# Two transformer blocks on one core: most of the 128x128 transposes taken off TensorE and done by VectorE in 32x32 blocks with a trip through DRAM

## What is computed

```
h   = rmsnorm(x);  proj = h @ w_in                      # 2048 -> 9216
u, v_sgu, q, k, v, g_a, g_b = split(proj)
y_a = gelu(u) * spatial_gating(rmsnorm(gelu(v_sgu)))    # 8 groups of 128
y_b = stick_breaking_attention(rmsnorm(q), rmsnorm(k), v)   # 8 heads
x  += (sigmoid(g_a)*(y_a @ w_up_a) + sigmoid(g_b)*(y_b @ w_up_b)) @ w_o
x  += (silu(gate)*up) @ w_ffn_out,   [gate, up] = rmsnorm(x) @ w_ffn_in   # 5632 wide
x  += sigmoid(rmsnorm(x) @ w_ple_gate) * (p @ w_ple)
# second block
z   = rmsnorm(x) @ w_in2                                # 3584 columns: conv, pool, q
kv  = rmsnorm(mem) @ w_kv
x  += concat(conv(z), pool(z), attention(q, kv)) @ w_out
u   = causal_dwconv(rmsnorm(x) @ w_up2, 3 taps) + bias  # 2 x 5632 columns
x  += (silu(gate)*val) @ w_down
out = rmsnorm(x)
```

## Time and profile before

| what | value |
|---|---|
| time, median of 3 runs (lowest to highest) | 2510.04 us (2508.74 to 2510.11) |
| time of the profiled execution itself | 2509.36 us |
| its span, first to last instruction | 2507.2 us |
| TensorE busy | 2486.9 us, 99% |
| VectorE busy | 1403.4 us, 56% |
| ScalarE busy | 1244.4 us, 50% |
| DMA, mean of 16 engines | 62.2% on the queue of the weights, 189 GB/s |
| granted TensorE clock | 0.999 of full |

### The profile page before, as it was taken

One profiled execution on the slowest core, in us unless ns is written; L12 is line 12 of the kernel. 1 busy time (PEld: TensorE's weight loads), 2 busy tenths in 40 slices (PEclk: granted clock), 3 DMA queues, 4 the chain that ended last, 5 costly groups with the idle time before them and its releaser, 6 DMA issues.

```text
span 2507.2 us, 27926 instructions
## 1 busy us (share of the span) xinstructions
PE 2486.9 (99%) x11322; PEld 2065.1 (82%) x11322; DVE 1403.4 (56%) x1668; ACT 1244.4 (50%) x1531; POOL 0.2 (0%) x4
## 2 busy tenths in 40 slices
PE   9999999999999999999999999999999999999998
PEld 7888888888888888888888788888888888888886
DVE  7564555655555455544445654765566665665544
ACT  7554666445444444444445654444555555554443
POOL 0000000000000000000000000000000000000000
PEclk9999999999999999999999999999999999999999
DMA  8656666666666666666666565566666666666663
GB/s 287 185 180 188 193 187 178 192 185 185 187 191 189 189 190 188 192 186 192 192 189 225 171 186 178 168 190 186 180 191 185 184 184 191 185 184 209 194 193 128
DMA packets 131105, 473.55 MB, mean 189 GB/s; under 512 B 14624, under 2 KB 15008, under 8 KB 130720
## 3 DMA queue, kind: packets, MB, share of 16 engines
q1 hardware_dynamic: 130976, 471.77, 62.2%
HBM read 469.61 MB, written 2.10 MB: 188 GB/s over the span
## 4 chain that ended last, share of the span: by engine, by line
PE 98%; ACT 1%; DVE 1%; DMA 0%; issue 0%; SPq 0%; DVEq 0%; ACTq 0%
PE ps L1291 86%; PE ps L1297 8%; PE ps L374 2%; ACT wh L1327 0%; DMA raw<-in_w_in 0%; DVE wl L1328 0%; PE ps L732 0%; PE ps L703 0%; PE ps L748 0%; PE ps L580 0%; PE ps L958 0%; PE ps L994 0%; DVE X L881 0%; DVE tmp L876 0%; PE ps L705 0%
## 5 line engine op out<-in xcount | busy, mean ns | idle before, releaser
L1328 DVE TENSOR_TENSOR wl<-raw,wh 128x1024 fp32r<-128x1024 f32 x877 | 1074.0, 1225 | 1076.9 <-ACT wh L1327 1076.6
L1327 ACT CAST wh<-raw 128x1024 fp32r<-128x1024 f32 x877 | 922.6, 1052 | 1171.4 <-PE ps L1297 1168.1
L1291 PE MATMUL ps<-wh,x1g_hi 128*128 128x512 f32 x704 | 276.1, 392 | 0.0
L1291 PE MATMUL ps<-wh,x4g_hi 128*128 128x512 f32 x704 | 276.0, 392 | 0.0
L1291 PE MATMUL ps<-wh,act_hi 128*128 128x512 f32 x704 | 274.3, 390 | 0.0
L1291 PE MATMUL ps<-wl,x1g_hi 128*128 128x512 f32 x704 | 274.0, 389 | 0.0
L1291 PE MATMUL ps<-wl,x4g_hi 128*128 128x512 f32 x704 | 273.9, 389 | 0.0
L1291 PE MATMUL ps<-wl,act_hi 128*128 128x512 f32 x704 | 273.9, 389 | 0.0
L1291 PE MATMUL ps<-wh,h_hi 128*128 128x512 f32 x576 | 227.0, 394 | 2.3 <-DVE wl L1322 1.3
L1291 PE MATMUL ps<-wl,h_hi 128*128 128x512 f32 x576 | 224.1, 389 | 0.0
L1291 PE MATMUL ps<-wh,x1g_lo 128*128 128x512 f32 x528 | 205.7, 390 | 0.0
(11 more groups left out here) (271 smaller groups left out, 3147.4 us busy)
## 6 DMA issues: line engine op xcount, KB each, us to landing
raw<-in_w_in SPq DMA_DIRECT2D x200, 512.0 KB, 3.6
raw<-in_w_ffn_in SPq DMA_DIRECT2D x176, 512.0 KB, 3.6
raw<-in_w_up SPq DMA_DIRECT2D x176, 512.0 KB, 4.2
raw<-in_w_ffn_out SPq DMA_DIRECT2D x88, 512.0 KB, 3.6
raw<-in_w_down SPq DMA_DIRECT2D x88, 512.0 KB, 3.6
raw<-in_w_o SPq DMA_DIRECT2D x32, 512.0 KB, 3.6
raw<-in_w_ple_gate SPq DMA_DIRECT2D x32, 512.0 KB, 3.6
raw<-in_w_out SPq DMA_DIRECT2D x32, 512.0 KB, 3.6
```

Of the source, the lines that this page charges most:

```text
L1291: return e.matmul(*a, start=s, stop=p, skip_group_check=True)
L1327: hi = act.do(lambda e, r=r, slot=slot: e.copy(wh[:, r, :], raw[:, slot, :]), in_tok[s], free)
L1328: lo_tok[s] = dve.do(lambda e, r=r, slot=slot: e.tensor_tensor(wl[:, r, :], raw[:, slot, :], wh[:, r, :].bitcast(F32), ALU.subtract), hi)
```

## The change

- `turn` no longer uses TensorE. Two VectorE instructions transpose the 32x32 blocks of the chunk's rows into a new buffer `Y` [128 x 1024]; one DMA on GpSimd's queue writes `Y` to a DRAM scratch tensor `rows` (two of them in turn, 512 KB each); GpSimd's queue waits for that, and four more DMAs (one for each group of 32 partitions, 128 KB each in pieces of 1 KB) read it back into a new buffer `Z` so that every feature lies on its partition. The VectorE instructions wait until the previous turn's write has left `Y`, the four reads until the previous turn's readers are done with `Z`.
- The readers take their tiles from `Z` in SBUF, through strided views with pieces of 32 elements, in two halves of 128 tokens each. They stand later: step +6 in `unfold` (turn at +1), +7 in `after_u` and `after_z` (turn at +1), +10 in `after_qk` (turn at +4), +8 in `after_ub` and `after_ffn1` (turn at +1), +7 in `after_ffn2` (turn at +1).
- `turn_now` is the old way, kept for 5 turns of 67: the last chunk of `unfold` of three of the four norms, the last of `after_ub`, and chunk 6 of `after_z`.
- `after_ffn1` turns two chunks together (11 turns of 8 tiles in place of 22 of 4). `after_ffn2` first copies `Z` into `Y` on ScalarE (two instructions of 128x512), the taps then read `Y`.
- The two new buffers take 8 KB per partition, so RAW goes from 6 to 4. Some functions move by 2 to 5 steps (`sgu_pair`, `xhead`, `pool_tile`, `conv_taps`, `conv_split`), the order of `w_out`'s granules changes, and the first chunk of `after_ffn1`, `after_pgate` and `after_ffn2` is no longer 2 or 3 steps late.

```diff
-RAW = 6
+RAW = 4
...
-MIX_ORDER = (12, 14, 0, 6, 2, 8, 10, 4)
+MIX_ORDER = (12, 14, 0, 6, 8, 10, 2, 4)
...
+        Y = view("Y", [P, 1024], o_y)
+        Z = view("Z", [P, 1024], o_z)
+        YF = Y.rearrange("p (c t) -> p c t", c=4)
+        YQ = Y.rearrange("p (q g c j) -> p q g c j", q=4, g=2, c=4)
+        ZT = Z.rearrange("p (a g c j) -> p c g a j", a=4, g=2, c=4)
+        ZA = Z.rearrange("p (a e) -> p a e", a=4)
...
-        def turn(src, tok, bk, n):
-
-            done = None
-            for c in range(n):
+        turned = {"n": 0, "y": [], "z": []}
+        def turn(src, *tokens):
+            n = turned["n"]
+            turned["n"] += 1
+            for b in range(2):
+                done = dve.do(lambda e, b=b: e.transpose(YQ[:, :, b].rearrange("p q c j -> p c q j"),
+                                                         src[:, b, :].rearrange("p (c q j) -> p c q j", c=4, q=4)),
+                              *tokens, turned["y"])
+            there = moves.load(s_rows[n % 2], rows_out[n % 2], Y[:], done)
+            for q in range(4):
+                back = moves.load(s_turn[n % 4], ZA[32 * q:32 * q + 32],
+                                  rows_out[n % 2, :, 256 * q:256 * q + 256].rearrange("(a i) e -> i a e", a=4),
+                                  there, turned["z"])
+            turned["y"] = there
+            turned["rows"] = done
+            return back
+        def split_turned(dest, c, tok):
+            for h in range(2):
+                hi_, lo_ = (tiles(x[:, c:c + 4, :])[:, :, h] for x in (dest.hi, dest.lo))
+                hi = act.do(lambda e, o=hi_, h=h: e.copy(o, ZT[:, :, h]), tok)
+                lo = dve.do(lambda e, o=lo_, i=hi_, h=h: e.tensor_tensor(o, ZT[:, :, h], i.bitcast(F32), ALU.subtract), hi)
+            turned["z"] = lo
+            for k in range(c, c + 4):
+                dest.ready[k] = lo
+        def turn_now(src, tok, bk):
+            for c in range(4):
                 for b in range(2):
                     at_ = (c % 2) * T + b * P
                     done = pe.do(lambda e, c=c, b=b, at_=at_: e.transpose(
                         ps[:, bk + c // 2, at_:at_ + P], src[:, b, c * P:(c + 1) * P], ident[:]),
-                        tok, bank_free[bk], bank_free[bk + 1] if n > 2 else None, got_mats["ident"])
+                        tok, bank_free[bk], bank_free[bk + 1], got_mats["ident"])
             return done
-        def turned(bk, c):
+        def turned_tile(bk, c):
             return ps[:, bk + c // 2, (c % 2) * T:(c % 2 + 1) * T]
+        def tiles(x):
+            return x.rearrange("p c (g a j) -> p c g a j", g=2, a=4)
...
-            bk = 6 if norm is norm4 else 4 + 2 * (n % 2)
             g = {}
+            xs = X[:, :, 512 * n:512 * n + 512]
+            soon = n == 3 and norm is not norm4
 
             def a():
                 squares(n, tok, norm)
+                if not soon:
+                    g["t"] = turn(xs, tok)
 
             def b():
-                g["t"] = turn(X[:, :, 512 * n:512 * n + 512], tok, bk, 4)
+                if soon:
+                    g["t"] = turn_now(xs, tok, 6)
                 for i in range(4):
                     c = 4 * n + i
-                    hi = act.do(lambda e, c=c, i=i: e.activation(dest.hi[:, c, :], turned(bk, i), ACT.Copy,
-                                                                 scale=gain(gname, c)), g["t"], free())
-                    if i % 2 == 0:
+                    src = turned_tile(6, i) if soon else ZT[:, i:i + 1]
...
-            at(s + 2, b)
+            at(s + (2 if soon else 6), b)
...
-                    g["t"] = st_tok["free"] = turn(ST, g["st"], bk, 4)
+                    g["t"] = turn(ST, g["st"])
+                    st_tok["free"] = turned["rows"]
                 hi = act2.hi[:, 2 * n:2 * n + 2, :].rearrange("p k t -> p (k t)")
                 lo = act2.lo[:, 2 * n:2 * n + 2, :].rearrange("p k t -> p (k t)")
 
                 def a():
-                    g["c"] = [act.do(lambda e, c=c: e.activation(C[:, c, :], F[:, c, :], ACT.Identity,
+                    for h in range(2):
+                        g["f"] = act.do(lambda e, h=h: e.copy(tiles(YF)[:, :, h], ZT[:, :, h]), g["t"])
+                    g["c"] = [act.do(lambda e, c=c: e.activation(C[:, c, :], YF[:, c, :], ACT.Identity,
                                                                  scale=gain("fconv", 176 + 4 * n + c),
-                                                                 bias=gain("fbias", 4 * n + c)), g["t"], part_tok["tb"])
+                                                                 bias=gain("fbias", 4 * n + c)), g["f"], part_tok["tb"])
                               for c in range(4)]
+                    turned["z"] = g["f"]
 
                 def b():
                     g["o"] = []
                     for c in range(4):
                         o = dve.do(lambda e, c=c: e.scalar_tensor_tensor(
-                            C[:, c, 1:], F[:, c, 0:T - 1], gain("fconv", 88 + 4 * n + c), C[:, c, 1:],
+                            C[:, c, 1:], YF[:, c, 0:T - 1], gain("fconv", 88 + 4 * n + c), C[:, c, 1:],
                             ALU.mult, ALU.add), g["c"][c])
                         g["o"].append(o)
                     for c in range(4):
                         g["o"][c] = dve.do(lambda e, c=c: e.scalar_tensor_tensor(
-                            C[:, c, 2:], F[:, c, 0:T - 2], gain("fconv", 4 * n + c), C[:, c, 2:],
+                            C[:, c, 2:], YF[:, c, 0:T - 2], gain("fconv", 4 * n + c), C[:, c, 2:],
                             ALU.mult, ALU.add), g["o"][c])
-                    bank_free[bk] = bank_free[bk + 1] = [g["c"], g["o"]]
+                    turned["y"] = [g["c"], g["o"]]
...
-                w = 3 if n == 0 else 0
-                at(s + w, z)
-                at(s + w + 2, y)
+                z()
+                at(s + 1, y)
                 for i, fn in enumerate((a, b, c_, d, f, h)):
-                    at(s + w + 2 + i, fn)
+                    at(s + 7 + i, fn)
```

More of the change, by code:

```diff
@@ L230, in two_block_kernel @@
             "s_attn", "s_cst", "s_mats", "s_misc", "s_late", "s_mem", "s_out", "s_ident", "s_x", "s_gf"))
+        s_turn = [sem(f"s_turn{i}") for i in range(4)]
+        s_rows = [sem(f"s_rows{i}") for i in range(2)]
+        rows_out = nc.dram_tensor("rows", (2, P, 1024), F32, kind="Internal").ap()
         sp = Queue(sem("s_sp"))
@@ L402, in b @@
-                bank_free[bk] = bank_free[bk + 1] = [hi, dest.ready[c]]
+                    src = turned_tile(6, i) if soon else ZT[:, i:i + 1]
+                    as_src = (lambda v, c=c: v[:, c, :]) if soon else (lambda v, c=c: tiles(v[:, c:c + 1, :]))
+                    hi = act.do(lambda e, c=c, s=src, f=as_src: e.activation(f(dest.hi), s, ACT.Copy, scale=gain(gname, c)),
+                                g["t"], free())
+                    if soon and i % 2 == 0:
+                        first = (c, src, as_src)
+                        continue
@@ new lines, in b @@
+                    for c, src, as_src in ((first, (c, src, as_src)) if soon else ((c, src, as_src),)):
+                        for h in range(1 if soon else 2):
+                            half = (lambda v: v) if soon else (lambda v, h=h: v[:, 0, h])
+                            dest.ready[c] = dve.do(lambda e, c=c, s=src, f=as_src, h=half: e.scalar_tensor_tensor(
+                                h(f(dest.lo)), h(s), gain(gname, c), h(f(dest.hi).bitcast(F32)), ALU.mult, ALU.subtract),
+                                hi)
@@ L547, in b, with c @@
                 def b():
[L548 to L552, removed]
[L553 to L554 removed]
+                    g["t"] = turn(rows, g["u"])
+                    rows_tok[n] = turned["rows"]
+                def c():
+                    u_tok[n] = turned["z"] = [act.do(lambda e, h=h: e.copy(tiles(U[:, 4 * n:4 * n + 4, :])[:, :, h],
+                                                                           ZT[:, :, h]), g["t"]) for h in range(2)]
+                a()
+                at(s + 1, b)
+                at(s + 7, c)
             return after
@@ L638, in f, with h @@
                 def f():
[L639 to L644, removed]
+                    g["t"] = turn(rows, g["r"])
+                    rows_tok[n] = turned["rows"]
+                def h():
+                    turned["z"] = [act.do(lambda e, h=h: e.activation(tiles(dst[:, 4 * n:4 * n + 4, :])[:, :, h],
+                                                                      ZT[:, :, h], ACT.Copy, scale=g_ap),
+                                          g["t"], got_mats["gq"]) for h in range(2)]
+                    qk_tok.append(turned["z"])
                 a()
@@ L782, in after, with now @@
                 m = dve.do(lambda e: e.tensor_tensor(ST, ST, SG[:, n, :, :], ALU.add), tok, ua_tok[n])
+                g = {}
                 def a():
-                    done = st_tok["free"] = turn(ST, m, bk, 4)
```

(13 more changed lines are left out.)

108 lines of the change are left out of this document (59 added, 49 removed).

## The result

| | before | changed |
|---|---|---|
| median of 4 runs | 2509.46 us | 2567.64 us (2564.22 to 2573.86) |
| ratio | | 1.0235, 95% interval 1.0214 to 1.0255 |
| the profiled execution, and its span | 2509.36, 2507.2 us | 2573.86, 2572.0 us |

The change makes the kernel 2.3% slower, where 2460 us were forecast. It is the rival on the other side: the round trip became the bound of `w_up2`. The profiled execution of the changed kernel is the slowest of its four, 6.2 us above their median; the kernel before repeats within 1.4 us, the changed one within 10 us.

The account below looks back on a forecast made before the run. It took TensorE's instruction stream as the bound: 2509.4 - 56.9 (transposes) - 3.4 (a wait in the ple stage) + 7 (loop) + 3 (`w_out`'s start) = 2459.1, forecast as 2460 us; range 2449 to 2500 us.

Parts of the forecast that it names:

- the rival on the other side: In `after_ffn2`, the DMA trip becomes the bound and the change loses, for example 2528 us at 14.5 us; chance 12%.
- The loop: In `after_ffn2`, turn, trip, copies, taps, next turn once a chunk: 10.9 us plus R against 21.77; about 7 us lost.
- R: The DMA round trip, from the end of the transposes to the landing of the fourth read.
- I take R = 11.2 us: Trip estimate: 5.5 us for the write, as loads of `X`, and 5.7 for the reads, as `BS`.
- The bounds of 7.2 and 19.8: Trip limits: two legs of 3.6 us below; two of 9.9 us, as the 2 MB load, above.
- the 2452 without a loop: Whole kernel's time in us if the trip is hidden, R up to 10.9; that rival's chance 30%.
- hidden altogether: Rival: R up to 10.9, no loop in `after_ffn2`; 2452 us, or 2449 if `w_out`'s start is free; 30%.
- the other stages cost nothing: Trips in `unfold`, `after_z`, `after_u` and `after_qk` costed at nothing; `unfold` allowed about 16 us before TensorE stands.
- the cushion of 5 us: In `unfold`, ring slack of some 5 us beyond the 11.0 us of trip allowed for nothing.
- The weights rival: With four raw buffers, loads beside trips come late, 1 to 2 us in each of 62 turns; about 2490 us; 7%.
- The point of no gain: In `after_ffn2`, the loop takes back the 57.3 us won, 2.7 us in each of 21 periods, from R = 13.6.
- The 3 us for the start of `w_out`: Around `w_out`'s start, conv products, taps and pool splits come closer together on VectorE: 3 us (0 to 6).

Follow-up runs that it names:

- experiment 5: The changed kernel, with each weight load of `w_up2` fetching 64 of 1024 columns (wrong weights, same instructions and waits): 2472.20 us, ratio 0.9855.
- experiment 6: The changed kernel with taps reading a separate copy, placed behind the next chunk's turn in `w_up2`, plus 64-column weight loads there: 2473.03 us, ratio 0.9853.
- experiment 2: The kernel before, with RAW = 4 in place of 6 and nothing else: 2508.97 us, ratio 0.9999.
- experiment 3: The changed kernel, with the two VectorE transposes of each turn in `w_up2` made twice: 2548.11 us, ratio 1.0160.
- experiment 9: The changed kernel, with the weight load issued ahead of each `w_up2` trip's write held until that write has landed: 2542.84 us, ratio 1.0135.
- experiment 8: The changed kernel with `w_up2` turned on TensorE, and the readers of `unfold` at step +8 in place of +6: 2468.40 us, ratio 0.9838.
- experiment 1: The changed kernel, with the 22 turns of `w_up2` made on TensorE as before and taps reading PSUM: 2481.07 us, ratio 0.9887.
- experiment 4: The changed kernel, with the taps' copy in its own memory and the VectorE taps behind the next chunk's turn in `w_up2`: 2493.95 us, ratio 0.9933.

## Why the prediction was wrong, point by point

**Right.** TensorE was the bound, and its transposes cost what was read: without them a chunk of `w_up2` takes 21.77 us where nothing else interferes (experiments 5 and 6). A transpose pair on VectorE takes 1.30 us (1.3 taken). RAW = 4 costs the kernel before nothing (experiment 2). The loop is there, its fixed part is 10.94 us (10.9 taken), and it binds when R exceeds 10.9: periods of 21.76 us at R = 8.4, 26.48 at 15.5.

**Wrong: the size of R.** The step that failed is "I take R = 11.2 us". It was 15.6 in the loop shown, 15.5 in the median. Both legs were too small: 6.2 us for the write in place of 5.5, and 9.2 for the reads in place of 5.7; 0.3 us lie between the transposes and the write. The bounds of 7.2 and 19.8 held, and so did the arithmetic of the loop: 21 x (26.5 - 21.77) = 99 us on top of the 2452 without a loop gives 2551.

Beside small loads the legs are 3.25 and 5.1 us, R is 8.6 us (experiment 5); so 7.0 of the 15.6 us are the weights beside it. The reads were the larger miss, 3.5 of 4.4 us. I had taken four DMAs in a row from `BS`, which stood in the weights' own queue with small ones ahead of it. Here the four issues alone take 2.2 us, and the last landed 7.5 us after its issue. What was beside them is seen in the loads: seven were issued from 1956.0 to 1967.6, one in 1.9 us in place of 2.72, because ScalarE and VectorE catch up after each wait, just where the trip runs. I took this bunching at first for the whole cause, a late trip bunching the loads that make the next one late. That it is not: with the loop open the write leg was as long. Nor can it make most of R: beside `w_ffn_in`, where TensorE's pace is steady, R is 12.9 us, which is already 2.0 over the 10.9. By that R the loop would cost 21 x 2.0 = 42 us, an estimate; what is between 12.9 and 15.5 may be bunching or where the trip falls between two loads; no run parts these. Experiments 3 and 9 show what the write leg is worth: 3.2 to 3.5 us with the load ahead landed or about to, about 6 with it just begun. Experiment 9 also shows that this can't simply be had, since reads and weights then take part of it back.

The Trainium skill's figure for a DMA from GpSimd ("DMA: Bandwidth & Descriptors", Anatomy of one DMA: about 2.0 us and bytes/436e3, so an estimate of 3.2 us for 512 KB) agrees with the trace where only loads of 32 KB run beside it, 3.25 us. It does not hold beside the stream, 6.2 us. The R near 7 that I worked out from it would have put the change into the case "hidden altogether", and was not used in the sum.

**Wrong: the other stages cost nothing.** I let R be up to 16 us in `unfold` for nothing. Experiment 8 against 1 says 12.7 us between the medians; in the profiled execution of the changed kernel `w_up2` starts 20.2 us later than in that of experiment 8. The stage rows show where: between the first matmul of x2g and of x3g the kernel before took 153.2 us (1341.6 to 1494.8), the changed one 158.2, that of experiment 8 143.5. ScalarE waited up to 7.7 us for a trip, with its casts queued behind, and the cushion of 5 us that I had worked out for one wait did not hold in the ple stage. `w_ffn_in`, too, took 483.6 us in place of 489.1, while experiment 8 has 479.0, which is 22 x 21.77. TensorE has no gap in it from 620 us on, so the trips inside it cost nothing, as forecast, and the loss stands at its start, behind `unfold`. That the steps of the ple stage are fuller, with the split of `mem` put down in the same ones, is my reading; no run takes it apart.

**The weights rival** was in part right, and hidden by the loop. In the changed kernel ScalarE waited 49.6 us for the raw weights of `w_up2`, in gaps that the loop left anyway. With the loop opened it is what is left: 2494 us against 2473 with small loads, 21 us (experiments 4 and 6).

**The point of no gain was misplaced with it.** The prediction put it at R = 13.6, from 57.3 us won. Without the loop's loss the changed kernel takes 2472 us (experiment 5), so only 37 us were won, and the change loses from R = 10.9 + 37 / 21 = 12.7 us on. Experiment 9 fits that: R = 14.3 gives 2472 + 21 x 3.4 = 2543 us, and 2542.8 was measured.

**The sum by what the runs showed**, by place, against the profiled execution of 2573.9: 2449 without loop and extras, 20.2 ahead of `w_up2` (1738.1 against 1717.9 in experiment 8), 94.9 inside it (573.8 against 478.9), 8.5 behind it, makes 2573. The loop as a whole is 21 x (26.5 - 21.77) = 99 us from the first to the last turn; its last period ends behind the stage's last matmul, so a part of the 8.5 us is the same loss. The 3 us for the start of `w_out` were too much: from first to last start its matmuls take 91.0 us, 92.5 before with three groups of transposes among them, so about 1 us was lost.

## What to carry to other kernels

Work moved from the bounding engine to a path with a long latency stays free only as long as no loop through in-order queues that holds this path takes longer than the period: add up the ring once per period (here trip, taps, next turn), compare it with the period, and give the later work its own buffer and a place behind the next start. Do not price a DMA trip beside a stream by the stream's calm landings: it was 8.6 us beside small loads and 15.6 beside the weights. With four raw buffers the stream lost nothing without trips and 21 us beside them in the open loop; whether six would do there was not tried. The same move can be right in 40 places and wrong in 22; here leaving `w_up2` on TensorE and letting the readers stand two steps later turned +2.3% into -1.6%.

## What the runs showed of the hardware

- A 512 KB write issued 1.5 us after another queue's 512 KB load, and followed by the next such load 0.84 us later, took 5.9 us to land; with the load ahead 2.8 us old and about to land, and the same load behind, 3.1 us; with the load ahead 1.5 us old and the next one 1.6 us behind, 3.6 us. So neither load alone decides it. Why was not tried.
- Each DMA on GpSimd's queue holds that queue 0.55 us, so four reads take 2.2 us to issue.
- Transposing 128x512 float32 in 32x32 blocks takes VectorE 0.686 us, as much as a two-operand instruction of that size (0.684 us), with the result written through a strided view.
- Behind a wait of TensorE of over 1 us the first matmul took 0.50 to 0.80 us in place of 0.39, and the mean granted clock over the stage was 0.95 of full (0.985 over the run), in stretches at one half between longer ones at full. The ring's sum gives the period without it, so in this stage it cost nothing that the trace shows.
